# Gate projections computed as Strassen block products over 1024 tokens, in stages of their own, with turned x and ungated rows kept in DRAM

## The reference

```
h = rmsnorm(x, ln_gain);  proj = h @ w_in            # w_in: 2048 x 5376
A: 16 query heads of 64, 2 kv heads, banded window attention with sinks and relative bias
B: o_c = b * causal_conv3(c * xh)                    # 512 channels
M: 4 heads of 128, attention into 256 memory tokens
mixed = concat(silu(g_a)*o_a, silu(g_c)*o_c, silu(g_m)*o_m)    # 1024 + 512 + 512
out = x + mixed @ w_out                              # w_out: 2048 x 2048
```

## Time and profile before

| what | value |
|---|---|
| median of 3 runs | 2679.17 us |
| the profiled execution | 2680.0 us, span 2678.1 us |
| granted PE clock, mean | 0.999 |
| PE busy | 2656.4 us, 99% |
| DVE, POOL, ACT busy | 64%, 56%, 41% |
| mean DMA rate | 143 GB/s |

### The profile page before, as it was taken

The page is one execution under the profiler, slowest core; times in us unless marked ns, Lnnn a source line. Parts: engine busy times, 40 slices in busy tenths (PEclk is TensorE's granted clock), DMA queues, the critical chain, the costliest instruction groups (busy, mean ns, idle before and its releaser), DMA issues.

```text
span 2678.1 us, 33671 instructions
## 1 busy us (share of the span) xinstructions
PE 2656.4 (99%) x12476; PEld 2194.0 (82%) x12476; DVE 1727.3 (64%) x2496; ACT 1093.2 (41%) x2400; POOL 1505.8 (56%) x1042
## 2 busy tenths in 40 slices
PE   7999999999999999999999999999999999999999
PEld 6888887888888888888887888888788888888887
DVE  4357676774577678357666864666534887858677
ACT  6333434442344344233434442343443444444443
POOL 6556554556564445566444555564445675756666
PEclk9999999999999999999999999999999999999999
DMA  8345433544534354444433534533355554544533
GB/s 256 119 140 161 133 104 109 179 128 143 166 111 134 102 160 139 142 142 150 130 106 116 168 126 141 173 108 121 96 173 175 162 174 142 173 146 145 173 124 136
DMA packets 233560, 383.16 MB, mean 143 GB/s; under 512 B 15718, under 2 KB 75188, under 8 KB 231348
## 3 DMA queue, kind: packets, MB, share of 16 engines
q1 hardware_dynamic: 188612, 274.05, 34.1%
q10 hardware_dynamic: 44784, 106.96, 11.4%
HBM read 308.86 MB, written 46.92 MB: 133 GB/s over the span
## 4 chain that ended last, share of the span: by engine, by line
PE 88%; DVE 6%; issue 2%; ACT 1%; DMA 1%; POOL 1%; SPq 0%; ACTq 0%
PE acc L1535 22%; PE acc L1537 21%; PE acc L1536 21%; PE acc L1602 3%; PE acc L1606 3%; PE acc L1604 3%; DVE early L1059 2%; DVE ungated L1314 1%; PE ps_s L1667 1%; DVE a_lo L1408 1%; PE ps_o L1685 1%; PE ps_s L1659 1%; DMA raw<-in_w_mem_kv 1%; PE ps_s L1602 1%; PE ps_z L1606 1%
## 5 line engine op out<-in xcount | busy, mean ns | idle before, releaser
L554 POOL TENSOR_TENSOR w_lo<-raw,w_hi 128x512 fp32r<-128x512 f32 x928 | 1313.7, 1428 | 1142.3 <-ACT w_hi L639 1139.7
L639 ACT ACTIVATE w_hi<-raw 128x512 fp32r<-128x512 f32 x928 | 571.5, 629 | 1069.2 <-PE acc L1537 773.6
L1535 PE MATMUL acc<-h_hi,w_hi 128*128 128x512 f32 x1792 | 705.1, 393 | 0.5
L1537 PE MATMUL acc<-h_hi,w_lo 128*128 128x512 f32 x1792 | 697.9, 389 | 0.0
L1536 PE MATMUL acc<-h_lo,w_hi 128*128 128x512 f32 x1792 | 697.9, 389 | 0.0
L1535 PEld LDWEIGHTS acc<-h_hi,w_hi 128*128 128x128 f32 x1792 | 336.3, 188 | 77.3 <-POOL w_lo L554 1.9
L1537 PEld LDWEIGHTS acc<-h_hi,w_lo 128*128 128x128 f32 x1792 | 336.3, 188 | 70.7
L1536 PEld LDWEIGHTS acc<-h_lo,w_hi 128*128 128x128 f32 x1792 | 336.4, 188 | 68.2
L1535 PE MATMUL acc<-w_hi,h_hi 128*128 128x512 f32 (+1 forms) x1024 | 379.4, 370 | 0.0
L1537 PE MATMUL acc<-w_hi,h_lo 128*128 128x512 f32 (+1 forms) x1024 | 372.0, 363 | 0.0
L1536 PE MATMUL acc<-w_lo,h_hi 128*128 128x512 f32 (+1 forms) x1024 | 371.4, 363 | 0.0
(11 more groups left out here) (233 smaller groups left out, 3609.7 us busy)
## 6 DMA issues: line engine op xcount, KB each, us to landing
raw<-in_w_in SPq DMA_DIRECT2D x336, 512.0 KB, 4.1
raw<-w_sums SPq DMA_DIRECT2D x64, 512.0 KB, 4.2
probs_t<-blocks_t SPq DMA_DIRECT2D x384, 64.0 KB, 2.1
raw<-in_w_out SPq DMA_DIRECT2D x48, 512.0 KB, 3.6
stage<-in_w_out ACTq DMA_DIRECT2D x16, 1024.0 KB, 5.7
w_sums<-stage ACTq DMA_DIRECT2D x16, 1024.0 KB, 5.5
stage<-in_x ACTq DMA_DIRECT2D x16, 1024.0 KB, 5.1
mixed_rows<-ungated ACTq DMA_DIRECT2D x12, 1024.0 KB, 4.2
```

The costliest lines, as they stand in the source:

```text
L554: nc.gpsimd.tensor_tensor(w_lo[:, at, :], raw[:, slot_mod, HALF * half:HALF * half + HALF], w_hi[:, at, :].bitcast(F32), ALU.subtract).the ...
L639: nc.scalar.activation(w_hi[:, 2 * (slot_mod % 2) + half, :], raw[:, slot_mod, HALF * half:HALF * half + HALF], ACT.Copy).then_inc(hi_read ...
L1535: nc.tensor.matmul(dst, st[0], mv[0], start=first, stop=False)
L1537: return nc.tensor.matmul(dst, st[1], mv[0], start=False, stop=last)
```

## The change

- The gate blocks leave the groups: a group is KV, A0, A1, M, C, X, B = 52 slots. Each is part of 4 new pairs of 28 slots (`gating(r)`), in which the left operand is turned x (with its gain) and the right one the gate columns; the weights are the stationary side. The order is two gate pairs and two output pairs for tokens 0 to 1023, then the same for 1024 to 2047. 8 pairs, 224 slots.
- A gate pair ends in ACT's tanh, DVE's `gate` (12 scalar_tensor_tensor with both tensors in SBUF, at positions 21, 26 and 5 of the next pair, and 4 out of PSUM at 13) and POOL's `mix` (16 multiplications, at 13, 14, 21, 22, 26, 27, 5, 6).
- Turned x goes to DRAM (`h_rows`), by 4 transposes of 128x512 a tile, in all four groups (the last turns group 0 again), with the gain multiplied in by a 128x2048 `x_gain` on DVE, and is loaded from there for the next group's split and for the gate pairs, in rows of 512 bytes. Ungated rows are stored to `half_rows` and loaded for the gate pairs.
- Queries: 12 transposes of 128x512 a group, and four DMAs by SP that put the 32-row blocks in place, for each of three query blocks.
- The units' places: L at every second slot from 17 to 47, and M at 34, 36, ... 48, between the L units of the second half.
- The weight sums are twice as many (8 tiles a group) and POOL makes them, two of four subtractions in each of two slots, at 8 and 9, 13 and 14, ... 44 and 45. ACT scales x and squares the queries; the convolution's first tap goes to ACT.

```diff
-BLOCKS = ["KV", "QM", "QA0", "QA1", "C", "X", "B", "GM", "GC"]
+BLOCKS = ["KV", "QA0", "QA1", "QM", "C", "X", "B"]
+GROUP_SLOTS = KV_SLOTS + SB_SLOTS * (len(BLOCKS) - 1)
-USES = len(BLOCKS) + LAST_GATES
+USES = len(BLOCKS)
+MEAN_AT = {12: 0, 20: 1, 28: 2}
+SCALE_AT = {13: 0, 22: 1, 29: 2}
+Q_TURN_AT = {13: (0, 0, 4), 24: (1, 0, 1), 26: (1, 3, 4), 30: (2, 0, 2)}
+Q_TURN_UNIT = {25: (1, 1, 3), 31: (2, 2, 4)}
+UNIT_AT = {17 + 2 * c: ("A", 0, c) for c in range(8)}
+UNIT_AT.update({33 + 2 * c: ("A", 1, c) for c in range(8)})
+UNIT_AT.update({34 + 2 * n: ("M", n // 2, n % 2) for n in range(8)})
+SPLIT_AT = {s + 2: u for s, u in SCORES_AT.items() if UNIT[u][0] == "A"}
+VALUES_AT = {s + 3: u for s, u in SCORES_AT.items()}
+CONV_AT = {46: 0, 48: 1, 49: 2, 50: 3}
-PAIRS = 4
+PAIRS = 8
+GATE_COLUMNS = ((G_A, G_A + 512), (G_C, G_M))
+GATE_AT = {21: "c22", 26: "c21"}
+MIX_AT = {13: ("c11", 0, 2), 14: ("c11", 2, 4), 21: ("c22", 0, 2), 22: ("c22", 2, 4),
+          26: ("c21", 0, 2), 27: ("c21", 2, 4)}
+LAST_TANH_AT, LAST_GATE_AT, LAST_MIX_AT = 1, 5, {5: (0, 2), 6: (2, 4)}
+X_FLIP_AT = {5: (0, 0, 4), 14: (1, 0, 4), 22: (2, 2, 3), 30: (3, 2, 4)}
+X_FLIP_UNIT = {21: (2, 0, 2), 23: (2, 3, 4), 29: (3, 0, 2)}
+X_GAIN_AT = {6: 0, 15: 1, 23: 2, 30: 3}
+H_SPLIT_AT = {46: (0, 1), 47: (2, 3), 48: (4, 5), 49: (6, 7), 51: (8, 9)}
+H_SPLIT_NEXT = {0: (10, 11, 12, 13), 1: (14, 15)}
+T_SUM_AT = {s + d: (n, 2 * (d - 1)) for s, n in T_LOAD_AT.items() for d in (1, 2)}
...
+        def gating(r):
+            return r % 4 < 2
...
+            def t_sum(g, n, first):                       # POOL
+                if first == 0:
+                    pool.wait_ge(t_in, 32 * (SB_SLOTS * g + n + 1))
+                    nc.gpsimd.tensor_tensor(b11, b12, b11, ALU.subtract).then_inc(t_step, 1)
+                    nc.gpsimd.tensor_tensor(b12, b22, b12, ALU.subtract).then_inc(t_step, 1)
...
+            def mix(r, block, first, end):                # POOL
+                    nc.gpsimd.tensor_tensor(to, gates[:, t, :], to, ALU.mult).then_inc(mixed, 1)
...
             def x_flip(g, n, first, end):                 # DVE
+                for q in range(first, end):
+                    last = nc.vector.transpose(
+                        x_blocks.rearrange("p (j k a) -> p j k a", j=4, k=KT)[:, :, 4 * q:4 * q + 4, :],
+                        xt[:, 512 * q:512 * q + 512].rearrange("p (k c j) -> p j k c", k=4, j=4))
+            def x_gain(g, n):
+                nc.vector.tensor_tensor(rows, rows, gain_of[:, :].unsqueeze(2).broadcast_to(
+                    [P, 4 * KT, 32]), ALU.mult).then_inc(x_gained, 1)
...
+            def gate(r, block):                           # DVE
+                for t in range(TT):
+                    dve.wait_ge(tanh_ready, done + t + 1)
+                    nc.vector.scalar_tensor_tensor(
+                        out=gates[:, t, :], in0=stage[:, t, :], scalar=1.0, in1=gates[:, t, :],
+                        op0=ALU.add, op1=ALU.mult).then_inc(gated, 1)
...
+                        if gating(r):
+                            st, mv = (w_hi[:, at, cols], w_lo[:, at, cols]), (hi, lo)
+                        else:
+                            st, mv = (hi[:, cols], lo[:, cols]), (w_hi[:, at, :], w_lo[:, at, :])
```

More of the change, by code:

```diff
@@ L308, in program @@
         q_turned = sem("q_turned")
+        q_in = [sem(f"q_in{kind}") for kind in range(3)]
         k_squared = sem("k_squared")
@@ L597, in _ @@
                               q_rstd)
+                    if s in T_SUM_AT:
+                        t_sum(g, *T_SUM_AT[s])
             def add_resid(r, to, t, made, loaded):
                 pool.wait_ge(sums_read, READS_A_PAIR * r + made)
[L602 removed]
+                pool.wait_ge(stage_in, 64 * nth_pair(r) + loaded)
                 nc.gpsimd.tensor_tensor(to[:, t, :], to[:, t, :], stage[:, t, :],
                                         ALU.add).then_inc(resid_added, 1)
+            def mix(r, block, first, end):
+                quarter, rows = gated_rows(r, block)
+                gates = {"c11": stage, "c22": u3, "c21": p1, "c12": u2}[block]
+                if first == 0:
+                    pool.wait_ge(half_in[quarter + 4 * (block[1] == "2")], 16 * (r // 4) + 16)
+                for t in range(first, end):
+                    if block == "c11":
+                        pool.wait_ge(sums_read, READS_A_PAIR * r + 4 + t + 1)
+                    else:
+                        pool.wait_ge(gated, GATE_ADDS * nth_pair(r) + GATED_COUNT[block] + t + 1)
+                    to = rows[:, 4 * quarter + t, :]
+                    nc.gpsimd.tensor_tensor(to, gates[:, t, :], to, ALU.mult).then_inc(mixed, 1)
             for j in range(OUT_SLOTS):
@@ new lines, in t_load @@
+                for half in range(2):
+                    if g < 2:
+                        src, col = w_in, GATE_COLUMNS[g][half]
+                    else:
+                        src, col = w_out, 1024 * (g - 2) + 512 * half
+                    act.dma_start(stage[:, :, :].rearrange("p (h n) c -> p h n c", h=2)[:, :, half, :],
+                                  src[:, col:col + 512].rearrange(
+                                      "(h k p) c -> k p h c", h=2, p=P)[n]).then_inc(t_in, 16)
@@ L898, in _ @@
                             a_high(s - GROUP_SLOTS + 2, h)
-                    if not last and s in H_SPLIT_AT:
-                        for k in H_SPLIT_AT[s]:
+                    if g:
+                        for k in H_SPLIT_NEXT.get(s, ()):
+                            h_high(g - 1, k)
+                    if not last:
+                        for k in H_SPLIT_AT.get(s, ()):
                             h_high(g, k)
@@ L934, in _ @@
-                if not last:
-                    for k in H_SPLIT_END:
-                        h_high(g, k)
+                    if s in ROWS_STORE_AT:
+                        rows_store(g, ROWS_STORE_AT[s])
+                    if g:
+                        for quarter in ROWS_STORE_NEXT.get(s, ()):
+                            rows_store(g - 1, quarter)
+                    if s in H_STORE_AT:
+                        h_store(g, H_STORE_AT[s])
+                    if s in X_LOAD_AT:
+                        x_load(g, X_LOAD_AT[s])
```

901 lines of the change are left out of this document (497 added, 404 removed).

## The result

| | before | after |
|---|---|---|
| median | 2679.34 us (2678.82 to 2679.73, 4 runs) | 2781.34 us (2777.41 to 2783.38, 4 runs) |
| ratio | | 1.038 (1.037 to 1.039) |
| span of the profiled execution | 2678.1 us | 2778.2 us |
| mean granted PE clock | 0.999 | 0.980 |
| matmul records | 12476 | 12092 |

The change is slower by 102 us; 2643 us and a range up to 2676 had been forecast. The matmuls went as planned: 12476 - 12092 = 384 records, 16 slots of 24. The span is 2778.2 - 2591.1 = 187.1 us above the floor, where the forecast had 51.

The account below looks back on a forecast made before the run. PE, busy 99% of the span, was taken as the bound. Floor 2591.1 + 5 + 24 + 6 + 3 + 13 = 2642.1 us of span, forecast 2643 us; 8-of-10 range 2600 to 2676, own range 2615 to 2670.

Parts of the forecast that it names:

- the floor: Whole kernel: 464 slots become 448 at 5.44 us each, attention matmuls unchanged, so 2678.1 falls to 2591.1 us.
- its own rule, the terms at double: Range of the forecast case: terms at a third and at double, stated as 2615 to 2670 us.
- Slots 28 to 32: DVE's list behind L unit 29 makes its low part late for PE: +1.5 us a group, 6 in all.
- Stores and moves "taken at 0": Group transfers and SP's 12 extra query DMAs a group: no cost to PE, at most 4 us a group.
- DMA and list order: Rival, 11%: a store ACT must await, or late rows of turned x, holds ACT and the weight halves: 2675 us.
- POOL at 12 to 14: POOL's power operations, weight sums and weight halves just fit two slots: taken at 0, at most 2 us a group.
- pairs 2 and 6: Third and seventh pairs: s2_tiles sums and the previous pair's last gate share slots; only in gate pairs' upper bound, 36 us.
- Group end: Positions 45 to 51: DVE's list runs late, PE waits 8 us in three groups: +24 us, bounds 0 to 45.
- Gate pairs: From position 21 DVE's gates and sums run late for slot 24: 13 us over four pairs, bounds 0 to 36.
- X evacuation: Behind slot 43 DVE starts it only after an M turning, late for slot 44: +3 us over four groups.
- DVE becomes the bound: Rival, 9%: sharing with POOL stretches gate pairs to 174 to 202 us each, giving 2770 us.
- the pairs' edges: Between pairs: 1.3 us over the 28 slots comes four more times, +5 us, bounds 0 to 10.

Follow-up runs that it names:

- e9: Changed kernel with query moves behind the probabilities, eight h_lo tiles on POOL, and turned-x stores issued by SP instead of ACT: 2811.4 us.
- e14: Changed kernel with replanned lists and h_lo tiles on POOL; weight-sum subtractions cut to 8 of 512 columns, gain to 64 of 2048: 2709.1 us.
- e11: Kernel before the change, with DVE held up ahead of one L unit's low part in each group so PE waits four times: 2709.1 us.
- e4: Changed kernel with 18 extra matmuls ahead of the values of L units 6 and 7, filling PE's wait: 2778.8 us.

## Why the prediction was wrong

The floor was right (448 slots, no attention matmul more), and each wait of the sum came. What failed is the sum of 51 us above the floor, where 187 were measured: it had waits at four places only, took the DMA lists and POOL at 0 and had no term for the clock. The range did not help: by its own rule, the terms at double, it would have ended at 2591.1 + 102 = 2693 and not at 2670, and 2781 lies above either.

**1. Slots 28 to 32: "Slot 29's end is 0: softmax ends at about 8" (+1.5 a group, measured 4.6).** Unit 6's values came due 4.63 us before 640.34, so slot 29 ended at about 635.7 - 18.5 = 617. The softmax began at 621.5, because in DVE's list it stands behind pt_lo of unit 5, and that waited until 620.9 for a transfer. Its turning ended at 630.3, 13 us behind the slot and not 8. A unit is a chain: softmax and turning 5.9, the move 4.7 (2.5 for SP's four issues, 2.2 to land, the medians of the run after), pt_hi and pt_lo 1.3, then the next softmax: 11.9 of the 12.2 us between two L units. In the kernel before the same wait stood in a row that I had quoted: pt_lo waits 5.37 us. I had counted that time as room (7.4 of 12.2 used). Between turning and pt_lo there are 5.3 us, 4.5 without the output sum; unit 6 has 8.7 us of other work there, 4.2 too many.

**2. Stores and moves "taken at 0" (measured 29 us).** Unit 3's 10.1 and unit 7's 18.9 are the rival "DMA and list order" that had 11%. For stores I had priced landings, and not the stand of ACT or SP until DVE has made the data, plus 0.6 to 3 us an issue. The Trainium skill (DMA: Bandwidth & Descriptors, "Anatomy of one DMA — SWDGE (gpsimd) path") says, of DMAs that POOL issues, that any semaphore wait happens on the sequencer that issues them, before dispatch. The runs show the same for ACT and SP: ACT idles 6.85 us ahead of a store in the run after, and the same stores in SP's list cost 62 us in e9. That rival's working, 1 us for each weight-sum tile, was the wrong place.

**3. POOL at 12 to 14 and in the slots beside units "at 0" (13.5 us of w_lo, and more).** Empty sums price the whole at 23 to 26 us. The meetings with POOL that the prediction weighed do lengthen DVE's operations (`a_lo` 1.16 us in the mean, 0.69 alone), but the 16 us of e14 were reached by less DVE work alone; how the 23 us divide between the longer DVE operations and POOL's own lateness was not separated beyond the waits above.

**4. The clock: no term (45 us).** I took a wait to cost itself. The 22 stretches at half clock cost 45 us beside PE's waits. That is 0.36 us for each of the 125 us of wait that came on top; e11 gives 0.34, and in e4 the stretch goes where the wait goes. The Trainium skill (TensorE: Matmul & The Clock Gate, "HAM oscillation — how this bites in real kernels") has this: a PE that pauses between groups of matmuls falls back to 1.2 GHz and pays again each time. The trace agrees, with a granted clock of 0.50 at every wait over 4 us.

**5. Start of the products, pairs 2 and 6: partly in the bounds, not in the sum (20 us).** 6.3 at the start (ACT in its loads), 5.64 + 2.85 us in pair 2, 5.65 in pair 6 (at 5.64 ACT's `a_hi` had waited 9.0 us for POOL's last mixes). These output pairs last 165.7 and 162.7 us for 153.6.

**What was right.** Group end: 24 us forecast, 21 measured, behind slots 48 to 50 as named, nearly gone with h_lo on POOL, and absent in the last group, which has none; the part that was to show at the first KV slot did not come. Gate pairs: 13 forecast; 0.5 + 0.36 + 2.09 a pair, 12 in all, near position 24. X evacuation 3, measured 5.7. "DVE becomes the bound" gave about the right total (2770) by a wrong mechanism, which is luck: it wanted 174 to 202 us a gate pair, and those behind the first last 157.6 to 157.7, just above the 153 to 157 of the forecast; the first lasts 169, with the 6.3 us of the start in it.

Together: 46 us of forecast waits were 57 in the same places, 71 came at places taken at 0 or only in the bounds, and 45 are clock. Of the some 15 us left, 5 were forecast as the pairs' edges; where the rest lies was not looked into.

## What to carry to other kernels

Idle time of an engine in a list is room only at the place where it idles: follow one unit's chain across engines (here 11.9 of 12.2 us) before adding work or taking slots away. Every DMA that an engine issues counts its wait for the data, with all that stands behind it. PE's stops cost here a third more than their length. Fewer matmuls bought nothing here, because the engines beside PE had to do nearly the same work in less time: the best version here that leaves nothing out took 2748.3 us, still 2.6% over the kernel before.

## What was not expected of the hardware

Behind a wait of 2.3 us in e11 PE kept full clock, behind 4.6, 6.1 and 9.1 us it ran at half for about 3, 4.5 and 6 us; but waits of 2.09 us in the gate pairs of the run after brought half clock four times out of four. Issuing the four DMAs of a query block took SP 4.1 to 5.1 us as a rule and 8.0 to 8.6 beside four stores of ACT. Extra DRAM-to-DRAM copies of 1 MB cost 1.2 us each, their issue by ACT (0.8 in the mean) included, though the DMA engines were busy only 0.59 of the span; cutting reads gave nothing. Not settled: what holds unit 7 (3.5 us) and the M queries' evacuation (3.1 us) in a group of e14, where sums and gains are empty and a group still lasts 340.5 to 343 us against 321.9.
